# PEER experts on one core: all U rows first, then half of V's columns multiplied densely and half gathered

## What is computed

```
q = (hblk @ w_q).reshape(..., PEER_HEADS, 2, PEER_QDIM // 2)
s1 = einsum('bthd,hnd->bthn', q[..., 0, :], k1);  s2 = einsum(..., q[..., 1, :], k2)
v1, i1 = top_k(s1, 16);  v2, i2 = top_k(s2, 16)
cand = v1[..., :, None] + v2[..., None, :]
cidx = i1[..., :, None] * 128 + i2[..., None, :]
score, pos = top_k(cand, 16);  idx = take_along_axis(cidx, pos)
gate = softmax(score)
act = gelu(einsum('bthkd,btd->bthk', w_u[idx], hblk))
out = einsum('bthk,bthkd->btd', gate * act, w_v[idx])
```

## Time and profile before

| | us |
|---|---|
| median of three runs | 2938.45 (2937.06 to 2939.99) |
| span of the profiled execution | 2939.0 |
| first expert row issued | 1622.0 |
| first U product on DVE | 1631.9 |
| last V row issued | 2912.3 |
| busy over the span: PE, DVE, ACT, POOL | 2628.4, 1949.4, 979.2, 556.7 |
| moved from and to memory | 901.77 MB, of which 604.02 MB through POOL's queue |

### The profile page before, as it was taken

One profiled execution on the slowest core, in us unless ns is written; L12 is line 12 of the kernel. 1 busy time (PEld: TensorE's weight loads), 2 busy tenths in 40 slices (PEclk: granted clock), 3 DMA queues, 4 the chain that ended last, 5 costly groups with the idle time before them and its releaser, 6 DMA issues.

```text
span 2939.0 us, 30782 instructions
## 1 busy us (share of the span) xinstructions
PE 2628.4 (89%) x11045; PEld 1777.7 (60%) x11045; DVE 1949.4 (66%) x2654; ACT 979.2 (33%) x1335; POOL 556.7 (19%) x580
## 2 busy tenths in 40 slices
PE   7999998999999999999999897777878877777777
PEld 3588886888777899998888753332434333232232
DVE  4679997444676788887555866666556656556646
ACT  5577776433564443334444211111101111111110
POOL 0000000000000000000000453433333333333333
PEclk9999999999999999999999999999999999999999
DMA  8733334542425888887566899999999999999998
GB/s 351 278 108 114 114 129 158 189 170 101 154 90 233 332 322 335 322 336 279 203 247 266 357 422 421 421 421 421 421 421 421 421 421 421 421 421 422 422 421 342
DMA packets 126356, 901.77 MB, mean 307 GB/s; under 512 B 14000, under 2 KB 15536, under 8 KB 17200
## 3 DMA queue, kind: packets, MB, share of 16 engines
q0 software_dynamic: 82944, 604.02, 49.8%
q1 hardware_dynamic: 38448, 276.84, 25.1%
q10 hardware_dynamic: 4864, 19.61, 1.7%
HBM read 898.29 MB, written 2.13 MB: 306 GB/s over the span
## 4 chain that ended last, share of the span: by engine, by line
PE 53%; DMA 35%; DVE 6%; issue 4%; ACT 1%; POOL 0%; POOLq 0%; SPq 0%; ACTq 0%; DVEq 0%
DMA u<-in_peer_u,idx 32%; PE ps L476 12%; PE ps L519 8%; PE ps L521 8%; PE ps L520 8%; PE ps L491 6%; DVE u L2042 3%; PE ps L882 2%; DMA v<-in_peer_v,idx 2%; PE ps L599 2%; PE ps L905 1%; DMA w<-in_stream 1%; PE ps L533 1%; PE ps L711 1%; PE ps L694 1%
## 5 line engine op out<-in xcount | busy, mean ns | idle before, releaser
L905 PE MATMUL ps<-v,dg 128*128 128x512 f32 x1920 | 894.4, 614 | 252.3 <-DMA v<-in_peer_v,idx 212.2
L2042 DVE SCALAR_TENSOR_TENSOR u<-u,hN 128x2048 f32<-128x2048 f32 x256 | 586.6, 2292 | 459.8 <-DMA u<-in_peer_u,idx 459.4
L905 PEld LDWEIGHTS ps<-v,dg 128*128 128x128 f32 x1920 | 356.4, 194 | 784.9 <-issue 427.9
L1383 DVE TENSOR_TENSOR wl<-w,wh 128x1024 fp32r<-128x1024 f32 x428 | 519.7, 1222 | 359.2 <-ACT wh L1018 358.8
L1018 ACT ACTIVATE wh<-w 128x1024 fp32r<-128x1024 f32 x428 | 451.3, 1059 | 607.9 <-PE ps L521 405.6
L2148 POOL DMA_INDIRECT u<-in_peer_u,idx x256 | 257.6, 1006 | 933.0 <-DVE u L2042 543.5
L476 PE MATMUL ps<-both,wh 128*128 128x256 f32 x2048 | 371.8, 284 | 0.0
L1326 ACT ACTIVATE dg<-con,wt 128x128 f32<-128x128 f32 x240 | 92.7, 399 | 807.4 <-PE ps L905 802.4
L476 PEld LDWEIGHTS ps<-both,wh 128*128 128x128 f32 x2048 | 320.1, 192 | 3.5 <-issue 3.3
L476 PE MATMUL ps<-both,wl 128*128 128x256 f32 x1024 | 289.8, 283 | 0.0
L2132 POOL DMA_DIRECT2D mr<-in_wmod x64 | 34.1, 534 | 1322.8 <-DVE br_lo L1791 912.7
(11 more groups left out here) (297 smaller groups left out, 2893.5 us busy)
## 6 DMA issues: line engine op xcount, KB each, us to landing
w<-in_stream SPq DMA_DIRECT2D x258, 1024.0 KB, 4.9
mr<-in_wmod POOLq DMA_DIRECT2D x64, 1024.0 KB, 6.9
wg<-in_gates ACTq DMA_DIRECT2D x8, 512.0 KB, 3.2
wx<-in_stream SPq DMA_DIRECT2D x4, 1024.0 KB, 7.9
u<-in_peer_u,idx POOLq DMA_INDIRECT x256
v<-in_peer_v,idx POOLq DMA_INDIRECT x256, 18.0
xs<-in_ctx ACTq DMA_DIRECT2D x1, 2048.0 KB, 7.6
xs<-in_x ACTq DMA_DIRECT2D x1, 2048.0 KB, 14.6
```

The source lines that it names most:

```text
L905: last = mm(ps[:, b, :], dg[:, k % 4, :], V[n % NV][:, b * 512:(b + 1) * 512], start=(k == 0), stop=(k == TOPK - 1))
L1383: tt(wl[p % SPLITS][:, :, :], W[s][:, q * PIECE:(q + 1) * PIECE, :], wh[p % SPLITS][:, :, :].bitcast(F32), ALU.subtract)\
L2042: stt(U[n % NU][:, :], U[n % NU][:, :], 1.0, hN[t][:, :], ALU.mult, ALU.mult, accum_out=dot[:, t, k:k + 1])\
```

## The change

All U rows come first, for both tiles, then V. The order of the halves becomes: head 0 of tile 0, head 0 of tile 1, heads 1 to 7 of tile 0, heads 1 to 7 of tile 1 (256 row tiles, r = 0 to 255; q = r // 16 is the half, k = r % 16). U has 8 buffers.

- In halves q >= 2 the row tiles with k = 3, 8, 13 (41 in all) are multiplied on POOL (`product`) and summed over the columns on ACT (`row_sum`). For the other row tiles of these halves, except q = 9, DVE reads hN from four PSUM banks, to which ACT has copied it (`spread_h`).
- The weights of a tile are made once for all 8 heads (128 columns).
- The left 1024 columns of V are not gathered. For each token n, DVE makes two 128x128 matrices: oa has a one where i1 of expert slot p is the column, ob has the slot's weight where i2 is the column (`onehot`). PE's product of the two is the token's weight for all 16384 experts, and ACT copies it from PSUM into WT (`store_weights`), 64 KB a partition for a tile. This is done for tile 0 during the U rows of tile 1 (`TOKEN_AT`), for tile 1 after them.
- Then PE multiplies WT with the left half of V, read densely: 128 loads of 128 rows by 1024 columns (0.5 MB each, issued by SP, 6 buffers), four matmuls of 512 columns a load (`dense`).
- The right 1024 columns are gathered by POOL in 256 transfers of 0.5 MB (4 buffers), and DVE multiplies by the weight and adds (`gathered`).

```diff
+ORDER = [(0, 0), (1, 0)] + [(0, h) for h in range(1, PH)] + [(1, h) for h in range(1, PH)]
+ON_POOL = tuple(r for r in range(2 * TOPK, ROWS) if r % TOPK in (3, 8, 13) and r != ROWS - 3)
+ROUTE_AT = (1, 2, 4, 6, 7, 9, 11, 12, 14)
+TURN0 = 9
+TOKEN_AT = {n: TURN0 * TOPK + 5 + n * 103 // P for n in range(P)}
...
-        NU, NV = 4, 8
+        NU, NG, ND = 8, 4, 6
...
 (SP)
+            for j in range(NKEYS):
+                if j == 0:
+                    sp.wait_ge(*AR.at(PH - 1, "q"))
+                elif j == 2:
+                    sp.wait_ge(*PR.at(2 * PH - 1, "s"))
+                elif j == 4:
+                    sp.wait_ge(*VG_.at(1, "g1"))
+                elif j >= ND:
+                    sp.wait_ge(dense_done, j - ND + 1)
+                sp.dma_start(VD[j % ND][:, :], a_vd[j]).then_inc(vd_in[j % ND], 16)
...
 (PE)
+            def token(t, n):
+                m = t * P + n
+                pe.wait_ge(onehots, m + 1)
+                if m % 4 == 0 and m >= 8:
+                    pe.wait_ge(w_stored, m // 4 - 1)
+                mm(ps[:, (4, 7)[m // 4 % 2], n % 4 * P:(n % 4 + 1) * P], oa[m % 6][:, :], ob[m % 6][:, :], start=(n % 4 == 0), stop=True,
+                   skip_group_check=True).then_inc(w_made, 1)
+            def dense(j):
+                pe.wait_ge(vd_in[j % ND], 16 * (j // ND + 1))
+                for t in (0, 1):
+                    for b in range(DB):
+                        last = mm(ps[:, DB * t + b, :], WT[t][:, j, :], VD[j % ND][:, b * 512:(b + 1) * 512], start=(j == 0), stop=(j == NKEYS - 1))
...
+            tables(1)
+            for n in range(P):
+                token(1, n)
+            pe.wait_ge(w_stored, 2 * P // 4)
+            for j in range(NKEYS):
+                dense(j)
...
 (ACT)
+            def spread_h(t):
+                fn(ps[:, 0:4, :].rearrange("p b n -> p (b n)"), hN[t][:, :], ACT.Copy).then_inc(spread, 1)
+            def row_sum(r):
+                act.wait_ge(pool_products, pool_by(r))
+                fn(U[r % NU][:, :], U[r % NU][:, :], ACT.Copy, accum_out=dot[:, t, c:c + 1]).then_inc(act_dots, 1)
+            def store_weights(g):
+                t, n = divmod(4 * g, P)
+                act.wait_ge(w_made, 4 * g + 4)
+                fn(WT[t][:, :, n:n + 4].rearrange("p i t -> p t i"), ps[:, (4, 7)[g % 2], :].rearrange("p (t i) -> p t i", t=4), ACT.Copy).then_inc(w_stored, 1)
...
 (DVE)
+            def onehot(t, n):
+                m = t * P + n
+                if m >= 6:
+                    dve.wait_ge(w_made, m - 5)
+                tsc(oa[m % 6][:, :], iota_k[:, :], i1T[:, n:n + 1], None, ALU.is_equal)
+                tsc(ob[m % 6][:, :], iota_k[:, :], i2T[:, n:n + 1], wT[:, n:n + 1], ALU.is_equal, ALU.mult).then_inc(onehots, 1)
+            def gathered(m):
+                t, c = m % 2, m // 2
+                dve.wait_ge(vg_in[m % NG], 16 * (m // NG + 1))
...
+                    stt(acc[:, t, :], VG[m % NG][:, :], dot[:, t, c:c + 1], acc[:, t, :], ALU.mult, ALU.add).then_inc(summed, 1)
+            for r in range(ROWS):
+                q, k = divmod(r, TOPK)
+                t, h = ORDER[q]
+                if r not in ON_POOL:
+                    hv = hN[t][:, :] if q in (0, 1, TURN0) else ps[:, 0:4, :].rearrange("p b n -> p (b n)")
+                    dve.wait_ge(u_in[r % NU], 16 * (r // NU + 1))
+                    stt(U[r % NU][:, :], U[r % NU][:, :], 1.0, hv, ALU.mult, ALU.mult, accum_out=dot[:, t, h * TOPK + k:h * TOPK + k + 1])\
+                        .then_inc(dve_dots, 1)
+                if (q == 0 and k) or (q == 1 and k < 14) or (q > 1 and k in ROUTE_AT):
+                    next(routes, None)
+                if q == TURN0 and k == 1:
+                    gelu_inner_of(0)
+                if q == TURN0 and k == 3:
+                    weights_of(0)
+                if q == TURN0 and k == 5:
+                    copy_tables(0)
...
+                for n in range(P):
+                    if TOKEN_AT[n] == r:
+                        onehot(0, n)
+            gelu_inner_of(1)
+            weights_of(1)
+            copy_tables(1)
+            for n in range(P):
+                onehot(1, n)
+                if n % 8 == 7:
+                    gathered(n // 8)
+            for m in range(P // 8, ROWS):
+                gathered(m)
+            dve.wait_ge(m5_in, 16)
+            dve.wait_ge(summed, ROWS)
...
 (POOL)
+            def product(r):
+                t, _ = ORDER[r // TOPK]
+                pool.wait_ge(u_in[r % NU], 16 * (r // NU + 1))
+                nc.gpsimd.tensor_tensor(U[r % NU][:, :], U[r % NU][:, :], hN[t][:, :], ALU.mult).then_inc(pool_products, 1)
+            for r in range(ROWS):
...
+                if r >= NU:
+                    pool.wait_ge(*row_used(r - NU))
+                nc.gpsimd.indirect_dma_start(out=U[r % NU][:, :], ...)
+                if r - NU + 1 in ON_POOL:
+                    product(r - NU + 1)
+            for m in range(ROWS):
...
+                elif m >= NG:
+                    pool.wait_ge(summed, m - NG + 1)
+                nc.gpsimd.indirect_dma_start(out=VG[m % NG][:, :], ...)
```

More of the change, by code:

```diff
@@ L399, in build, with dots_by, pool_by, row_used @@
+        def dots_by(r):
+            return sum(1 for n in range(r + 1) if n not in ON_POOL)
+        def pool_by(r):
+            return sum(1 for n in ON_POOL if n <= r)
+        def row_used(r):
+            return (act_dots, pool_by(r)) if r in ON_POOL else (dve_dots, dots_by(r))
+        PRIMED_V = [VT, VL] + VO + [VS, VW]
+        PRIMED_A = [AD, AL] + AO + [AS]
+        PRIMED_P = [PL]
         block = ctx.enter_context(nc.Block())
@@ new lines, in _ @@
+            load_queries(7, 5)
+            for q in range(5, 2 * PH):
+                load_keys(q)
+            for j in range(NKEYS):
[8 more added lines that the diff above has]
+                sp.dma_start(VD[j % ND][:, :], a_vd[j]).then_inc(vd_in[j % ND], 16)
+                if j == 24:
+                    sp.dma_start(m5r[:, :], m_dram[3:4, :].to_broadcast([P, D])).then_inc(m5_in, 16)
@@ new lines, in scores, with tables @@
+                pe.wait_ge(keys_in, q * 16)
+                for s in (0, 1):
+                    last = mm(ps[:, 5 + q % 2, s * NKEYS:(s + 1) * NKEYS], qT1[:, h, s, :] if t else qT0[:, (h + 1) % 6, s, :], keys[:, s, :],
+                              start=(s == 0), stop=True, skip_group_check=True)
+                last.then_inc(*PR.inc("s"))
+            def tables(t):
+                if t:
+                    pe.wait_ge(w_stored, P // 4)
+                pe.wait_ge(*VG_.at(t, "w"))
+                for i, x in enumerate((te[:, 0, t, :], te[:, 1, t, :], dot[:, t, :])):
+                    last = nc.tensor.transpose(ps[:, 4, i * P:(i + 1) * P], x, ident)
+                last.then_inc(turned_t, 1)
@@ new lines, in _ @@
+            queries(6)
+            scores(5)
+            queries(7)
+            for q in range(6, TURN0 + 4):
+                scores(q)
+            pe.wait_ge(*AR.at(PH - 1, "q"))
+            tables(0)
+            for q in range(TURN0, 2 * PH):
+                for n in range(P):
+                    if TOKEN_AT[n] // TOPK == q:
+                        token(0, n)
+                if q + 4 < 2 * PH:
+                    scores(q + 4)
+            tables(1)
+            for n in range(P):
+                token(1, n)
@@ L1321, in diagonals @@
-            def diagonals(h, t, routed=None):
-                act.wait_ge(*VE.at(h, f"w{t}"))
-                for k in range(TOPK):
-                    n = t * TOPK + k
-                    act.wait_ge(*(PE_.at(h, "v%d%d" % divmod(n - 4, TOPK)) if n >= 4 else PE_.at(h - 1, f"v1{TOPK - 4 + k}")))
-                    fn(dg[:, k % 4, :], ident, ACT.Copy, scale=wt[:, t, k:k + 1]).then_inc(*AE.inc(f"dg{t}{k}"))
-                    if k == 11 and routed is not None:
-                        gates(routed, t)
-                    if h == PH - 1 and k == 3:
-                        act.wait_ge(m5_spread, 1)
-                        fn(m5r[:, :], ps[:, 4:8, :].rearrange("p b n -> p (b n)"), ACT.Copy).then_inc(m5_in, 1)
@@ new lines, in _ @@
+            assert next(routes, None) is None
+            gelu_inner_of(1)
+            weights_of(1)
+            copy_tables(1)
+            for n in range(P):
+                onehot(1, n)
[5 more added lines that the diff above has]
+            dve.wait_ge(summed, ROWS)
+            for t in (0, 1):
+                tt(acc[:, t, :], acc[:, t, :], m5r[:, DC:D], ALU.mult).then_inc(*VX.inc(f"m{t}"))
+                dve.wait_ge(*VX.at(0, f"m{t}"))
+                tt(x2[:, t, DC:D], x2[:, t, DC:D], acc[:, t, :], ALU.add).then_inc(*VX.inc(f"o{t}"))
```

572 lines of the change are left out of this document (243 added, 329 removed).

## The result

The changed kernel takes 3068.64 us (median of 4 runs, 3066.33 to 3072.8) against 2938.48 (4 runs): ratio 1.0447, 95% interval 1.0432 to 1.0461, so 130 us slower. The prediction was 2963, range 2885 to 3020: right in sign, 106 us short, and the result lies outside the range. The profiled execution has a span of 3064.5.

A forecast was written before the change was run, and what follows sets the result against it. The prediction took DMA at 421 GB/s to bound the kernel before. Stage by stage, U ends at 2392, dense starts at 2479, V ends at 2949, and a tail of 14 gives 2963 us, range 2885 to 3020.

The forecast's parts named there:

- end of halves 0 and 1: First 32 U rows: DVE decides with 102 us against 99 of DMA, ending at 1734.
- halves 2 to 8: Next 112 U rows: DVE 40.2 us a half against 39.8 of DMA, 281 us in all, to 2015.
- halves 9 to 15 with the products' cost: Last 112 U rows with tile 0's one-hots: DVE-bound 317 us plus 60 for POOL's products, to 2392.
- to the first dense matmul: Between U and V: weights 5, tile 1's one-hots 61, gathered sums 18, slow PE clock 3; dense starts at 2479.
- V stage: Dense matmuls beside gathers: PE 440 us, DMA 446, gathers 478; 470 us taken, to 2949.
- gather loop: V's gathers with four buffers: round of 8.3 us, 2.08 a gather, 478 us for 236.
- Gather loop: Rival for V's gathers: held issues and 4 us landing make 2.4 us each, 566 for 236, total 3059; chance 0.08.
- The products' cost: DVE held by POOL's products through a shared SBUF way: 3 us each in halves 9 to 15, 60 us, bounds 0 and 84.
- POOL's own time: POOL's issues and products in U's halves: 16 x 1.24 + 3 x 4.8 = 34 us a half, not binding.
- Without the products 2332: End of U's last product if POOL's products cost DVE nothing: 2332 instead of 2392.
- Faster: Rival: POOL's products cost DVE nothing and gathers keep DMA full, 2879, or 2909 with half the 60; chance 0.33.
- Costly one-hots: Rival: one-hots 0.63 us a token, not 0.47, total 3003; POOL's 84 instead of 60 adds 24; within the 0.50 case.

The follow-up runs named there:

- experiment 1: Changed kernel with six buffers for gathered V rows instead of four and four for dense columns instead of six: 2995.72 us, ratio 1.019 to the kernel before.
- experiment 7: Changed kernel with POOL's products at other rows: two placements with further mends, 2959.15 and 2966.49 us; rows 0, 3, 8 alone, 3061.65 us.
- experiment 4: Changed kernel without POOL's 41 multiplications, those rows summed unmultiplied: 2981.07 us, ratio 1.0144 to the kernel before.

## Why the prediction was right in sign and wrong in size

By its own steps, predicted against the profile after:

| step | predicted | measured | difference of its length |
|---|---|---|---|
| end of halves 0 and 1 | 1734 | 1731.9 | -2 |
| halves 2 to 8 | 281 us, to 2015 | 303.7, to 2035.6 | +23 |
| halves 9 to 15 with the products' cost | 377, to 2392 | 385.3, to 2420.9 | +8 |
| to the first dense matmul | 87, to 2479 | 80.7, to 2501.6 | -6 |
| V stage | 470, to 2949 | 549.6, to 3051.2 | +80 |
| tail | 14 | 13.3 | -1 |

The forecast was 24 us slower, the result is 130; the sign itself had been given a chance of 0.58.

- **The step that failed is the gather loop.** It had every piece: 0.84 to POOL, issue, landing, 1.2 for the sum, an issue held by the next sum, four buffers, 8.3 / 4 = 2.08. The piece mis-sized is the landing: 5.3 us from the issue's start (0.94 + 2.4 + 1.95), 6.3 with the held issue, where the profile has a median of 7.5 in the dense stretch. The 2.4 of fixed time was from loads in stretches in which DMA was mostly 3 to 8 tenths busy. After dense is over, gathers alone land in 5.4 (median), so it is beside dense loads that the term fails; why a load takes longer there stays open. 9.8 / 4 = 2.46. This is the rival "Gather loop" in its mechanism: 4 us of landing beside the transfer, 2.4 each. That its 3059 is so near to 3068.64 is partly luck, for it has 566 us for the V stage, which took 550, and leaves out the 29 us by which U ended later. It got a chance of 0.08, and the range ended at 3020, below it. Two of the argument's numbers, 2.08 from the loop and 1.95 from what dense leaves, were close to each other; a loop so near the bound deserved a wider range.
- The rate of the V stage was nearly right: 408 GB/s with enough buffers, where 421 had been taken. The Trainium skill, DMA: Bandwidth & Descriptors, section iDMA fabric, has 408.7 for one stream of loads with rows of 4 KiB: by this figure 459 us, an estimate, and experiment 1's rate agrees with it to 0.2%; the V stage there, 480, still holds a tail of 41 us in which gathers run alone.
- **The products' cost** was right in kind (shared way, DVE held to the end of the product) and too small: 94 us for 41. In halves 9 to 15 it is 72 against the 60 predicted for 20 products, on top of 313 where 317 had been worked out. In halves 2 to 8 it is 20, where 1.8 a half had been taken for DVE, of which only 0.4 stood out above DMA's time: there the index steps and their masks lost 7 x 2.49 + 14 x (0.35 + 0.31) = 27 us, and DVE waited 7.5 us for late rows.
- **POOL's own time**, 34 us a half in the prediction, which "does not bind", left out the wait for ACT's sum behind each product: 41.3 us a half by the rows of experiment 7, above DMA's 39.8.
- "Without the products 2332": 2327 measured. The one-hots' 0.47 a token: 0.45 where nothing holds them (2226.73 to the next product at 2227.18). A sum's 1.14: 1.28. The product on POOL: 4.46 as the upper end, 4.52 measured. Dense 440: 439.7.
- **The rival "Faster"** asked for a free way and a full DMA. Neither held: experiment 4 has the price, experiment 1 the loop.
- **"Costly one-hots"**: only from PSUM did they cost 0.57 a token; held ones are the products' cost. The rival's own sum is off: 3003 and 24 more are 3027, above the 3020 that it calls the upper end.

So 29 us of the miss stood at the end of U, and 80 in the V stage, less 7 elsewhere: 102, with 2963 + 102 = 3065 against the span of 3064.5.

## What to carry to other kernels

When a loop of few buffers fetches from DMA beside another stream, price its round with the landing under that stream's load, and compare the round divided by the buffers with the share it needs: here 2.08 stood against 1.95 and the buffers decided: two more were worth 73 us. A change that reads 67 MB less of V lost all of it, and more, by serializing stages that had hidden each other, by a DVE bound in tile 1's halves and by 80 us with little to load; only with more buffers, most stalls taken out and fewer products on POOL did it come out 0.3% ahead. Before giving work to POOL, list which DVE instructions would stand beside it with two SBUF operands, or cast or compare one, and add to POOL's queue what each product keeps it from issuing: here 7.1 us, of which 2.8 are the wait for another engine to be done with the buffer that the next load refills.
